# Masking, scaling and taking the row maximum in one VectorE instruction per block, and two stick-breaking operations on GpSimd, in a kernel of attention mixers

## The reference, cut to what matters

```
MLA:     p = softmax(where(key <= query, s * scale, -inf))
window:  s = where(in_window, s * scale + bias, -inf)
         m = max(max(s), sink);  p = exp(s - m) / (sum(exp(s - m)) + exp(sink - m))
stick:   log_not = where(key < query, log_sigmoid(-z), 0)
         after   = cumsum(log_not, reverse) - log_not
         a       = where(key < query, exp(log_sigmoid(z) + after), 0)
each:    o = p @ v   (a @ v)
```

## Time and profile before

| | us |
|---|---|
| Median of three runs | 2006.38 |
| Lowest and highest | 2005.84, 2014.0 |
| The profiled execution | 2002.22 |
| Its span in the profile | 2000.4 |
| TensorE busy (matmuls) | 1839.9 (92%) |
| VectorE busy | 1425.0 (71%) |
| ScalarE busy | 932.1 (47%) |
| GpSimd busy | 137.2 (7%) |

### The profile page before, as it was taken

The page is one execution under the profiler, slowest core; times in us unless marked ns, Lnnn a source line. Parts: engine busy times, 40 slices in busy tenths (PEclk is TensorE's granted clock), DMA queues, the critical chain, the costliest instruction groups (busy, mean ns, idle before and its releaser), DMA issues.

```text
span 2000.4 us, 24149 instructions
## 1 busy us (share of the span) xinstructions
PE 1839.9 (92%) x9068; PEld 1490.0 (74%) x9068; DVE 1425.0 (71%) x1956; ACT 932.1 (47%) x1480; POOL 137.2 (7%) x264
## 2 busy tenths in 40 slices
PE   1699986789999999978999999999999999999997
PEld 0577865678887888767788878787878788877886
DVE  5668788767887788676778776567787765567554
ACT  1444344664445444655643364345433544445443
POOL 2011100001110111000011000000111000000000
PEclk9999998889999999986999999999999999999999
DMA  6789823049885898331589865445998563447552
GB/s 243 262 293 340 313 97 127 22 149 329 309 311 197 314 322 324 124 118 42 186 306 336 298 214 187 136 163 171 329 321 299 200 221 128 172 147 271 194 186 86
DMA packets 242299, 439.48 MB, mean 220 GB/s; under 512 B 16201, under 2 KB 156551, under 8 KB 241927
## 3 DMA queue, kind: packets, MB, share of 16 engines
q1 hardware_dynamic: 204810, 304.75, 45.2%
q0 software_dynamic: 36320, 131.13, 17.4%
q10 hardware_dynamic: 1052, 2.06, 0.3%
HBM read 436.79 MB, written 1.09 MB: 219 GB/s over the span
## 4 chain that ended last, share of the span: by engine, by line
PE 73%; DVE 14%; DMA 5%; ACT 5%; issue 3%; SPq 0%; DVEq 0%; ACTq 0%
PE bank L1592 22%; PE bank L1594 21%; PE bank L1593 21%; DVE weights_lo L972 4%; DMA arena<-in_w_ada 2%; DMA arena<-in_w_mod 2%; PE bank L1755 1%; DVE mod_acc L996 1%; DVE arena L1088 1%; DMA weights_raw<-in_w_ffn_gu 1%; DVE x L1152 1%; DVE arena L1146 1%; ACT weights_hi L561 1%; DMA weights_raw<-in_w_ffn_in 1%; DVE hT_lo L1097 1%
## 5 line engine op out<-in xcount | busy, mean ns | idle before, releaser
L972 DVE TENSOR_TENSOR weights_lo<-weights_raw,weights_hi 128x1024 fp32r<-128x1024 f32 (+2 forms) x584 | 672.6, 1199 | 175.6 <-ACT weights_hi L561 175.4
L1592 PE MATMUL bank<-weights_hi,hT_hi 128*128 128x512 f32 x1760 | 699.0, 397 | 31.6 <-DVE hT_lo L1097 20.0
L1594 PE MATMUL bank<-weights_hi,hT_lo 128*128 128x512 f32 x1760 | 686.6, 390 | 0.0
L1593 PE MATMUL bank<-weights_lo,hT_hi 128*128 128x512 f32 x1760 | 685.5, 389 | 0.0
L561 ACT ACTIVATE weights_hi<-weights_raw 128x1024 fp32r<-128x1024 f32 (+2 forms) x584 | 572.1, 1037 | 141.2 <-PE bank L1594 84.0
L1592 PEld LDWEIGHTS bank<-weights_hi,hT_hi 128*128 128x128 f32 x1760 | 332.9, 189 | 115.1 <-issue 27.9
L1594 PEld LDWEIGHTS bank<-weights_hi,hT_lo 128*128 128x128 f32 x1760 | 332.2, 189 | 69.7
L1593 PEld LDWEIGHTS bank<-weights_lo,hT_hi 128*128 128x128 f32 x1760 | 333.3, 189 | 64.0
L996 DVE SCALAR_TENSOR_TENSOR mod_acc<-arena,silu_cond,mod_acc 128x1024 f32<-128x1024 f32 x198 | 254.0, 1283 | 61.8 <-DMA arena<-in_w_mod 28.1
L704 ACT ACTIVATE actT_hi<-bank 128x512 fp32r<-128x512 f32 x66 | 39.5, 599 | 490.7 <-PE bank L1755 490.7
L1592 PE MATMUL bank<-weights_hi,actT_hi 128*128 128x512 f32 (+1 forms) x544 | 214.3, 394 | 7.4 <-DVE weights_lo L972 7.4
(11 more groups left out here) (277 smaller groups left out, 1312.2 us busy)
## 6 DMA issues: line engine op xcount, KB each, us to landing
weights_raw<-in_w_ffn_gu SPq DMA_DIRECT2D x176, 512.0 KB, 5.7
arena<-in_w_mod POOLq DMA_DIRECT2D x144, 512.0 KB, 6.6
weights_raw<-in_w_in SPq DMA_DIRECT2D x112, 512.0 KB, 4.7
arena<-in_w_ada POOLq DMA_DIRECT2D x96, 512.0 KB, 6.2
weights_raw<-in_w_ffn_down SPq DMA_DIRECT2D x88, 512.0 KB, 5.0
weights_raw<-in_w_ffn_in SPq DMA_DIRECT2D x88, 512.0 KB, 5.4
weights_raw<-in_w_ffn_out SPq DMA_DIRECT2D x44, 512.0 KB, 4.6
weights_raw<-in_w_out SPq DMA_DIRECT2D x32, 512.0 KB, 4.4
```

The costliest lines, as they stand in the source:

```text
L972: V.tensor_tensor(wlo[:, slot, 0:width], raw[:, slot, 0:width], whi[:, slot, 0:width].bitcast(F32), ALU.subtract).then_inc(S("lo_done"), 1)
L1592: T.matmul(o, sh, wh, start=start, stop=False)
L1593: T.matmul(o, sh, wl, start=False, stop=False)
L1594: return T.matmul(o, sl, wh, start=False, stop=stop)
```

## The change

In the loop, scale, mask and extreme become one instruction per block: `tensor_tensor_reduce` writes (scores + mask) * (-scale) and puts out the minimum of what it writes and of a start value, which is 3e38 for MLA heads and the negated sink for window heads. The stored scores are therefore negated, and the exponential gets scale -1. The window bias is multiplied by the square root of 64 once when it is built, since it is now added before scaling. The sinks are negated once per layer into a new tile. The product with the 0/1 mask and the addition of the 0/-1e30 mask move to GpSimd: the first between VectorE's L1424 and the running sums, the second ahead of the subtraction of the running sum in place of after it. VectorE waits for the latter. Three waits of VectorE on its own result go. On TensorE the two waits ahead of the transposes change places.

```diff
@@ -254,6 +254,7 @@
         latg = sb("latent_gains", [P, 3])
         kvhi = sb("latent_kv_hi", [P, 1, SEQ], F32R)
         kvlo = sb("latent_kv_lo", [P, 1, SEQ], F32R)
+        neg_sink = sb("neg_sinks", [P, WH])
         zero_hi = sb("zero", [P, 512], F32R)
         gate_t = sb("gate_bcast", [P, D])
         gate_r = sb("gate_rows", [8, P])
@@ -531,7 +532,7 @@
             for m in range(8 * MOD_CHUNKS[0][0]):
                 mod_load(m)
             f = 0
-            for k, (kind, _, _) in enumerate(phases, 1):
+            for k, (kind, _, a) in enumerate(phases, 1):
                 if kind == "ffn":
                     need(pool, S("x_done"), X_PARTS * k if k > 1 else 0)
                     units = list(range(8 * MOD_CHUNKS[f][0], 8 * MOD_CHUNKS[f][1]))
@@ -543,6 +544,12 @@
                     f += 1
                 else:
                     gate_bcast(k)
+                if kind == "mid1":
+                    for j in range(SH * a["l"], SH * (a["l"] + 1)):
+                        h = j % SH
+                        pool.wait_ge(S("soft_ready"), j + 1)
+                        nc.gpsimd.tensor_tensor(sb_u(h), sb_u(h), con[:, C_MASKS:C_MASKS + 384], ALU.mult).then_inc(S("stick_ready"), 1)
+                        nc.gpsimd.tensor_tensor(sb_z(h), sb_z(h), con[:, C_MASKA:C_MASKA + 384], ALU.add).then_inc(S("z_masked"), 1)
 
 
         @block.scalar
@@ -829,7 +836,7 @@
                         act.wait_ge(S("max_ready"), k + 1)
                         r = h % 2
                         for b, (c0, c1) in enumerate(((0, P), (P, 3 * P))):
-                            ins = nc.scalar.activation(sc_t[:, r, c0:c1], sc_t[:, r, c0:c1], ACT.Exp,
+                            ins = nc.scalar.activation(sc_t[:, r, c0:c1], sc_t[:, r, c0:c1], ACT.Exp, scale=-1.0,
                                                        bias=nmax[:, 2 * h + b:2 * h + b + 1], accum_out=rsum[:, 2 * h + b:2 * h + b + 1])
                         ins.then_inc(S("probs_ready"), 1)
                         if h >= MH:
@@ -1033,7 +1040,8 @@
                         ins = V.tensor_reduce(bias[:, :, c:c + 16], bank[4 + g][:, 0:288].rearrange("p (k q h) -> p h k q", q=3, h=WH), AX, ALU.add)
                     ins.then_inc(S("bias_taken"), 1)
                 dve.wait_ge(S("bias_taken"), 6)
-                V.tensor_tensor(bias[:, :, :], bias[:, :, :], con[:, C_MASKW:C_MASKW + 384].unsqueeze(1).broadcast_to([P, WH, 384]), ALU.add)\
+                V.scalar_tensor_tensor(bias[:, :, :], bias[:, :, :], HD ** 0.5,
+                                       con[:, C_MASKW:C_MASKW + 384].unsqueeze(1).broadcast_to([P, WH, 384]), ALU.mult, ALU.add)\
                     .then_inc(S("bias_taken"), 1)
 
             tr, turned = [0], [0]
@@ -1349,6 +1357,7 @@
                         ins = V.tensor_tensor(wq[:, t], wq[:, t], stat[:, 12 + 8 * t:20 + 8 * t].unsqueeze(2).broadcast_to([P, 8, HD]), ALU.mult)
                     then(ins)
                     dve.wait_ge(S("gains_loaded"), 16 * 5 * (l + 1))
+                    V.tensor_scalar(neg_sink[:, :], sink[:, :], -1.0, None, ALU.mult)
                     for t in range(NT):
                         V.tensor_tensor(wq[:, t, 0:WH], wq[:, t, 0:WH], gw64[:, 0:1, :].broadcast_to([P, WH, HD]), ALU.mult)
                         for kvh in range(WKV):
@@ -1410,26 +1419,22 @@
                         if m == 0 and h == MH:
                             dve.wait_ge(S("bias_taken"), 7)
                         scale = MQK ** -0.5 if h < MH else HD ** -0.5
-                        then(V.scalar_tensor_tensor(sc_t[:, r, :], bank[r][:, 0:384], scale, mask, ALU.mult, ALU.add))
-                        mx = nmax[:, 2 * h:2 * h + 2]
-                        V.tensor_reduce(mx[:, 0:1], sc_t[:, r, 0:P], AX, ALU.max)
-                        then(V.tensor_reduce(mx[:, 1:2], sc_t[:, r, P:384], AX, ALU.max))
-                        if h < MH:
-                            V.tensor_scalar(mx, mx, -1.0, None, ALU.mult).then_inc(S("max_ready"), 1)
-                        else:
-                            V.tensor_scalar(mx, mx, sink[:, h - MH:h - MH + 1], -1.0, ALU.max, ALU.mult).then_inc(S("max_ready"), 1)
+                        least = 3.0e38 if h < MH else neg_sink[:, h - MH:h - MH + 1]
+                        for b, (c0, c1) in enumerate(((0, P), (P, 3 * P))):
+                            ins = V.tensor_tensor_reduce(sc_t[:, r, c0:c1], bank[r][:, c0:c1], mask[:, c0:c1], -scale, least,
+                                                         ALU.add, ALU.min, nmax[:, 2 * h + b:2 * h + b + 1])
+                        ins.then_inc(S("max_ready"), 1)
                         if h < SH:
 
                             dve.wait_ge(S("sb_ln"), m + 1)
-                            then(V.scalar_tensor_tensor(sb_u(h), sb_z(h), 0.0, sb_u(h), ALU.max, ALU.add))
-                            V.tensor_tensor(sb_u(h), sb_u(h), con[:, C_MASKS:C_MASKS + 384], ALU.mult).then_inc(S("stick_ready"), 1)
+                            V.scalar_tensor_tensor(sb_u(h), sb_z(h), 0.0, sb_u(h), ALU.max, ALU.add).then_inc(S("soft_ready"), 1)
                         if 2 <= h < 2 + SH:
 
                             j = h - 2
                             z = sb_z(j)
                             dve.wait_ge(S("stick_sum"), SH * m + j + 1)
-                            then(V.tensor_tensor(z, z, bank[6 + j % 2][:, 0:384], ALU.subtract))
-                            V.tensor_tensor(z, z, con[:, C_MASKA:C_MASKA + 384], ALU.add).then_inc(S("zs_ready"), 1)
+                            dve.wait_ge(S("z_masked"), SH * m + j + 1)
+                            V.tensor_tensor(z, z, bank[6 + j % 2][:, 0:384], ALU.subtract).then_inc(S("zs_ready"), 1)
                         if h >= 9:
                             lo_static(n0 + 20 + h - 9, SLOT)
                         if h == 10:
@@ -1881,9 +1886,9 @@
                             T.matmul(bank[i % 2][:, P:384], q[:, P:SEQ], k, start=True, stop=True).then_inc(S("scores_ready"), 1)
                         if 1 <= i < 13:
                             h = i - 1
-                            pe.wait_ge(S("probs_ready"), 12 * m + h + 1)
                             if h >= 2:
                                 pe.wait_ge(S("pt_copied"), 12 * m + h - 1)
+                            pe.wait_ge(S("probs_ready"), 12 * m + h + 1)
                             for j in range(3):
                                 ins = T.transpose(bank[2 + h % 2][:, P * j:P * (j + 1)], sc_t[:, h % 2, P * j:P * (j + 1)], ident)
                             ins.then_inc(S("probsT_ready"), 1)
```

## The result

The changed kernel takes 1988.36 us in the median of 5 runs (1986.42 to 1989.94). The kernel before takes 2006.38 us in its own 5 (2004.77 to 2015.97). The ratio from the interleaved comparison is 0.9884 with a 95% interval of 0.986 to 0.9907; the two medians alone give 0.991, or 18 us less, where I had forecast 12. The sign was right, and so was the mechanism of the two loops. Two sizes were off: what a saved instruction is worth inside the loop, and how far the profiled execution stands from the median. The second is the step that failed.

The account below looks back on a forecast made before the run. The serial chain through both attention loops was taken to bound the kernel. Savings 3.2 + 3.2 - 0.2 + 6.5 = 12.7 us took the profiled 2002.22 to 1989.5; with 4.16 up to the median, 1994 us, range 1987 to 2008.

Parts of the forecast that it names:

- a ring of latency: Heads 5 to 8: scores, maximum, exponentials, transposes, scores two heads on; half of 0.5 us saved each, 1.0 in all.
- Mask, scale, extreme: Each head's path from scores to exponentials: fused pair takes 0.90 us instead of 1.41, so 0.5 us saved per head.
- My own alternative without the reads: Fused pair per head without separate accumulator reads: 0.70 us, about 0.2 us more saved per head.
- The loop: 3.2 us summed: First layer's attention loop: start 0.5, heads 3 to 4 0.7, heads 5 to 8 1.0, tail 1.0 us saved.
- The 0.7 for heads 3 to 4: Heads 3 to 4: VectorE's 3.43 us falls below TensorE's 2.68 us, saving 0.7 us.
- The tail: Loop end: heads 10 and 11 both stand in series with L1443, saving 2 x 0.5 = 1.0 us.
- GpSimd: 1.1 us taken: Stick-breaking operations of four heads on GpSimd: 1.1 us each, 2.2 a head, hidden behind TensorE, cost 0.
- The contention that I left out of the sum: GpSimd beside VectorE's additions L1424: up to 2 us a layer on the path, taken as 0.
- The clock: Second layer's loop: TensorE's granted clock stays at 2.4 GHz instead of falling, saving 6.5 us.
- Rivals 1 and 2: First: loops shorter, clock falls as before, 2000.9 us, chance 0.27; second: fused instruction no cheaper or engines exclude, 2005.4, 0.13.
- Rival 3: Running sums of heads 0 to 3: GpSimd's queue paces TensorE, clock rise fails; +12 us, 2018, chance 0.12.
- The median: Whole kernel: profiled time lies 4.16 us under the median; 1989.5 profiled therefore becomes 1993.7, stated as 1994.

Follow-up runs that it names:

- Fused alone: Changed kernel with both stick-breaking operations back on VectorE, fused instruction kept; median 1989.60 us, ratio 0.9914 against the kernel before.
- delayed kernel: Changed kernel plus two unused VectorE additions ahead of the fused instruction in heads 4 to 8; median 2017.39 us, ratio 1.0032 against the kernel before.
- GpSimd alone: Kernel before with only the stick-breaking operations moved to GpSimd, no fused instruction; median 1998.31 us, ratio 0.9948.

## Where the prediction was right, and the steps that failed

**What bounds the loops.** Right: a serial path through both loops, TensorE bound at heads 0 to 3 and 9 to 11, VectorE at heads 3 to 4, a ring of latency between. Fused alone shows which part is the cause.

**Mask, scale, extreme: 0.90 us taken, 0.64 measured.** This is the first mis-sized term. I had put 0.10 us on the path for each read of an accumulator, from ScalarE's row. VectorE starts its next instruction with the read. From the first mask instruction to the exponentials it is 0.68 us, 1.44 before, and the first transposes start 1.71 us after it in place of 2.48: 0.77 saved per head in place of 0.5. My own alternative without the reads (0.70) was nearer. The Trainium skill (VectorE: DVE Perf Modes, section on two Vector instructions with no wait between them) counts such an instruction as two; the trace does show two records each, but the second costs the path nothing.

**The loop: 3.2 us summed, 5.13 measured (first layer).** How far ahead the changed kernel is at each head's transposes, both counted from the first mask instruction:

| transposes of head | 0 | 2 | 3 | 4 | 5 | 6 | 7 to 10 | 11 | end |
|---|---|---|---|---|---|---|---|---|---|
| us ahead | 0.77 | 1.36 | 1.49 | 2.42 | 3.08 | 3.57 | 3.7 | 5.04 | 5.13 |
| my terms, added up | 0.5 | 0.5 | 0.5 | 1.2 | 1.4 | 1.7 | 2.2 | 3.2 | 3.2 |

The start is 0.3 larger for the reason above. Between heads 0 and 2 I had expected nothing, since TensorE is bound there. It is, but it starts sooner, and its clock rises 6 us into the loop instead of some 8: another 0.6. Heads 3 to 7 gave 2.4 where I had 1.7. The 0.7 for heads 3 to 4 came from the distance of two VectorE instructions in the earlier trace rows. What TensorE in fact stood for was the 0.63 us ahead of L1897, and behind it VectorE was still late for heads 4 and 5 because of L1431 and L1432. Heads 8 to 10 gave nothing, as they should at equal clock. The tail gave 1.3 where I had 1.0, again the price per head.

**GpSimd: 1.1 us taken, 1.0 measured, cost 0.** Right. The operations are hidden; doubled, they are not. The contention that I left out of the sum is real and hidden.

**The other small parts.** The order of waits is worth nothing, as I had said. For the negated sinks, 0.2 us, no row stands out, and nothing here could tell it.

**The clock: 6.5 us taken.** Right in the profiled pair, where the second loop kept its clock and gained 6.3 us more than the first. Filling the waits alone (8 us less) and putting waits back (the clock falls in both loops, 17 us more in them) show that it is a cause. Rivals 1 and 2 are refuted for this kernel: the clock does not fall in a loop of mixer 1 in either profile of the changed kernel, and the fused instruction is cheaper by half. Rival 3's waits exist and need twice the price; its +12 us did not come even then, the kernel being 6 us faster than before. What the two layers have in common before the fall was put too closely: they agree to 0.1 us up to head 6, not to 0.02.

**The median: the step that failed.** I added the same 4.16 us to the profiled time of the changed kernel that lay between profile and median of before. For the changed kernel the distance is -1.58 us: its profiled execution took 1989.94, close to my 1989.5, and its median is 1988.36. These 5.7 us are the whole way from 1994 to the measured median. The distance is not the same from kernel to kernel. Before, 22 runs of one session fall in two parts: those of 2004 to 2010 us have a mean granted clock of 0.969 to 0.971 (one 0.966), those of 2011 to 2017 one of 0.963 to 0.966. The profiled execution, at 0.971, was one of the better ones, with one fall. No run of the slower part was profiled, so that it had more or longer falls, and where, is inferred from its mean clock. With the waits of mixer 1's loops filled, that part is missing: 11 runs at 0.973 to 0.976. The changed kernel has no such spread either (1986.4 to 1989.9 us), and its profiled time is the top of it. So the kept clock was most likely worth more in the median than in the profiled pair, by the very mechanism that I had used. A profile shows one draw of a thing that is drawn anew in every run; the spread of the runs shown ahead of the prediction (2005.84 to 2014.0) held the hint.

Open is why the start of the first loop varies by 5.7 us between profiled executions (362.09 to 367.76 in versions that are alike up to there). The two latest starts, 367.76 and 367.56, are in the two profiles whose granted clock is 0.89 from 160 to 175 us, where all others have 1.00; why it fell there is not known.

## What to carry to other kernels

In a loop of small products look first for TensorE's waits, and price each twice: by its own length, and by what the granted clock does behind it, which in the second loop here was worth more. If the times of a kernel spread by more than its successor's could, the spread belongs to what can be won, so take the distance from profile to median from what varies, not as a constant. A fused VectorE instruction that also puts out an extreme costs what the reduction over its columns costs; price it by width and start to start, and count no read.

## What the runs showed of the hardware that was not expected

- An edit that shortened mixer 1's loops by 1.7 and 1.3 us cost the kernel 9 us in the median of 8 runs, each of them slower than every run of the changed kernel. In the one that was profiled the granted clock of mixer 2's loop, some 300 us behind, was 0.50 in place of 1.00. Three zero products in each of two waits there gave the loss back. The delayed kernel's profile shows the same fall in mixer 2, at a price of 11 us.
- TensorE stays at 1.2 GHz while it is busy without a gap: 22.15 of 22.20 us before, 22.82 of 23.00 in the delayed kernel. At 2.4 GHz it was busy for 22.02 of 24.00 us in the kernel with GpSimd alone and kept that level.
- Zero products in waits, which compute nothing, make a kernel faster: 7 us in the changed kernel, 8 in the one before.
- GpSimd's addition over 384 columns takes 0.99 us alone and 1.30 where it meets VectorE's addition of two SBUF tiles, which then takes 0.77 in place of 0.55. In the kernel with doubled operations two such meetings cost GpSimd 0.4 us and VectorE nothing.
